# A hybrid decoder layer in float32: shared weight tiles in the branch stage, six residual buffers, and the final norm inside the expert stage

## The reference

```python
def hybrid_mixer(x, ...):
    proj = x @ w_in
    ...
    o = gated_delta_rule(q, k, v, g, beta)
    o = o * rsqrt(mean(o ** 2) + EPS) * o_norm_g * silu(z)
    branch_a = o @ w_oa
    u = glu[..., :CONF_CH] * sigmoid(glu[..., CONF_CH:])
    u = causal_depthwise_conv(u, dw_w) + dw_b
    u = silu(layer_norm(u, cln_g, cln_b))
    branch_b = u @ w_ob
    h = sigmoid(gate_a) * branch_a + sigmoid(gate_b) * branch_b
    return h @ w_o

mix = hybrid_mixer(x, ...)
x = layer_norm(ALPHA * x + mix, ln1_g, ln1_b)
ffn = routed_experts(x) + shared_expert(x)   # 64 experts, 8 for each token
x = layer_norm(ALPHA * x + ffn, ln2_g, ln2_b)
```

## Time and profile before

| | |
|---|---|
| median of 3 runs | 2569.01 us (2566.07 to 2570.61) |
| the profiled execution | 2566.55 us |
| its span, first to last instruction | 2565.0 us |
| mean granted TensorE clock | 0.967 |
| TensorE busy | 2371.6 us, 92% |
| VectorE busy | 1752.2 us, 68% |
| ScalarE busy | 1311.6 us, 51% |
| GpSimd busy | 683.8 us, 27% |

### The profile page before, as it was taken

How to read it: one execution, slowest core, us unless ns; L and a number is a source line. 1 busy time by engine, 2 the same in 40 slices (tenths; PEclk the granted TensorE clock), 3 DMA queues, 4 the chain that set the end, 5 groups by cost and what they waited for, 6 DMA issues and landing times. The chain is left out here.

```text
span 2565.0 us, 40507 instructions
## 1 busy us (share of the span) xinstructions
PE 2371.6 (92%) x11611; PEld 1933.2 (75%) x11612; DVE 1752.2 (68%) x2295; ACT 1311.6 (51%) x1714; POOL 683.8 (27%) x674
## 2 busy tenths in 40 slices
PE   7999999999999999958999786899999998999995
PEld 6777778778877888846778574788888887888782
DVE  3436898898899766638646585577667777667645
ACT  3443654654565344334412143577677776667640
POOL 2001212112211111114002213444444443444330
PEclk9999999999999999978999898999999999999998
DMA  4335454333333453263764326799989999899935
GB/s 112 52 41 82 57 65 89 62 67 75 67 61 72 100 99 91 66 234 100 218 205 151 85 73 223 262 291 328 303 281 308 320 329 341 273 295 292 330 79 219
DMA packets 244142, 435.91 MB, mean 170 GB/s; under 512 B 25096, under 2 KB 149000, under 8 KB 244046
## 3 DMA queue, kind: packets, MB, share of 16 engines
q1 hardware_dynamic: 211198, 350.70, 47.1%
q0 software_dynamic: 32848, 83.96, 12.5%
HBM read 370.88 MB, written 97.71 MB: 183 GB/s over the span
## 5 line engine op out<-in xcount | busy, mean ns | idle before, releaser
L59 PE MATMUL dn_pj<-x_hi,dn_hi 128*128 128x512 f32 x1024 | 431.4, 421 | 1.8 <-PEq L84 1.8
L61 PE MATMUL dn_pj<-x_hi,dn_lo 128*128 128x512 f32 x1024 | 403.6, 394 | 0.0
L60 PE MATMUL dn_pj<-x_lo,dn_hi 128*128 128x512 f32 x1024 | 400.5, 391 | 0.0
L59 PE MATMUL gu_ps<-e_hi,xg_hi 128*128 (+1 forms) x752 | 311.8, 415 | 0.0
L2576 DVE TENSOR_TENSOR e_lo<-e_raw,e_hi (+1 forms) x128 | 292.3, 2285 | 22.5 <-ACT e_hi L2515 22.5
L61 PE MATMUL gu_ps<-e_hi,xg_lo 128*128 (+1 forms) x752 | 296.0, 394 | 0.0
L60 PE MATMUL gu_ps<-e_lo,xg_hi 128*128 (+1 forms) x752 | 295.0, 392 | 0.0
L2515 ACT ACTIVATE e_hi<-e_raw (+1 forms) x128 | 245.1, 1916 | 46.5 <-PEq L84 35.3
L61 PEld LDWEIGHTS dn_pj<-x_hi,dn_lo 128*128 128x128 f32 x1024 | 193.0, 188 | 44.3
L59 PEld LDWEIGHTS dn_pj<-x_hi,dn_hi 128*128 128x128 f32 x1024 | 194.2, 190 | 33.7 <-issue 2.9
L60 PEld LDWEIGHTS dn_pj<-x_lo,dn_hi 128*128 128x128 f32 x1024 | 194.5, 190 | 32.0 <-issue 1.0
(11 more groups left out here) (393 smaller groups left out, 5079.0 us busy)
## 6 DMA issues: line engine op xcount, KB each, us to landing
e_raw<-in_w_gate_e_dram SPq DMA_DIRECT2D x128, 512.0 KB, 5.5
e_raw<-in_w_up_e_dram SPq DMA_DIRECT2D x128, 512.0 KB, 8.4
e_raw<-in_w_down_e_dram SPq DMA_DIRECT2D x128, 512.0 KB, 7.8
dn_raw<-in_w_in_dram SPq DMA_DIRECT2D x64, 512.0 KB
gate_rows<-qkv_next SPq DMA_DIRECT2D x16, 512.0 KB, 3.1
br_raw<-in_w_oa_dram SPq DMA_DIRECT2D x16, 512.0 KB
br_gate<-gate_rows SPq DMA_DIRECT2D x32, 256.0 KB, 4.5
br_raw<-in_w_ob_dram SPq DMA_DIRECT2D x16, 512.0 KB
```

The lines of the kernel that those rows point to most:

```text
L59: nc.tensor.matmul(out, w_hi, x_hi, start=first, stop=False)
L60: nc.tensor.matmul(out, w_hi, x_lo, start=False, stop=False)
L61: return nc.tensor.matmul(out, w_lo, x_hi, start=False, stop=last)
```

## The change

Five edits.

1. The last store of o in the delta stage is issued by SyncE, ahead of the last gate store, and SyncE waits for it to land (`o_last`). GpSimd no longer issues it or waits for it.
2. The branch stage takes w_oa for both halves first: tiles 0 to 15 are column n // 2 of half n % 2, so a weight tile serves two products in turn; then w_ob for half 0 (16 to 23) and half 1 (24 to 31), loaded for each half as before. 24 weight tiles are loaded and split instead of 32. Both halves of o are loaded and split at the start (the second into the space of the squares), u's loads come behind. The statistics' matmuls move: the means behind tiles 4 and 11, the variances behind 9 and 17 (`MEAN`, `VAR`). `br_gated_a` holds all 1024 tokens, and h is made in it and stored from it.
3. In the shared stage there are six buffers for x instead of two: four more lie in the space of the gate and up tiles' split parts. SyncE loads blocks 0 to 5 ahead; loads 6 and 7 wait for the stores of blocks 0 and 1.
4. In the expert stage the two scatters ahead of the loop go. GpSimd raises the semaphores that they raised, and two more credit writes (0.5 KB) stand in for their landing.
5. The final norm is no stage any more: its loads, sums and norm stand at the end of the experts' streams, in the space of the weights' split parts. The parameters are loaded when the last weights have been split; y's loads wait for GpSimd's word that all scatters have landed (`all_in`). There are three accumulators instead of four. `end_stage` follows at the program's end.

The diff, cut to its core:

```diff
+                sp.wait_ge(o_fin, 1 + NG * NPAIR)
+                sp.dma_start(self.o_d[(NG - 1) * GH * P:, (NPAIR - 1) * 2 * P:].rearrange("(h p) t -> p h t", p=P),
+                             ob[:].rearrange("p (h t) -> p h t", h=GH)).then_inc(o_last, 16)
                 gate_store(4 * NPAIR - 1)
+                sp.wait_ge(o_last, 16)
...
-                    if p == NPAIR - 1 and not more:
-                        o_store(g, p)
...
-                pool.wait_ge(o_stored, 16 + NG * NPAIR * 16)
+                pool.wait_ge(o_stored, NG * NPAIR * 16)
...
-            oh, uc, sq = self.o_in, self.uc, self.cln_sq
+            uc, sq = self.uc, self.cln_sq
+            oh = [self.o_in, sq]
...
-            ha = sb(ctx, "br_gated_a", [P, KT, HALF])
-            ht = [sb(ctx, f"br_h{b}", [P, HALF]) for b in range(2)]
-            rstd = [sb(ctx, f"cln_rstd{t}", [P, HALF]) for t in range(2)]
+            ha = sb(ctx, "br_gated_a", [P, KT, S])
+            rstd = [sb(ctx, "cln_rstd", [P, HALF])] * 2
...
+            A_TILES = 2 * KT
...
-                return n // (2 * KT), n // KT % 2, n % KT
...
+                if n < A_TILES:
+                    return n % 2, 0, n // 2
+                return (n - A_TILES) // KT, 1, n % KT
+
+            def weight_of(n):
+
+                return n // 2 if n < A_TILES else n - KT
+
+            def last_use(w):
+
+                return 2 * w + 1 if w < KT else w + KT
+
+            def next_weight(n):
+
+                if n < A_TILES and n % 2 == 0 or weight_of(n) + 2 >= 3 * KT:
+                    return None
+                return weight_of(n) + 2
+
+            def weight_col(w):
+
+                return (0, w) if w < KT else (1, w % KT)
+
...
+            MEAN, VAR = (4, 11), (9, 17)
+            WO, H_TILES = 2 * KT + 5, 3 * KT + 4
...
+                    if n >= NGB + A_TILES:
+                        sp.wait_ge(h_ready, n - NGB - A_TILES + 1)
+                    elif n >= NGB:
                         sp.wait_ge(ps_read, n - NGB + 1)
...
+                    sp.dma_start(self.h_d[c * P:(c + 1) * P, hs[t]], ha[:, c, hs[t]]).then_inc(h_stored[c % 2], 16)
...
-                for t in range(2):
-                    sp.dma_start(uc[:, :, hs[t]], self.uc_d[:, hs[t]].rearrange("(k p) t -> p k t", p=P)
-                                 ).then_inc(uc_in[t], 16)
+                for i in range(2):
+                    o_part(1, i)
                 gate(0)
                 gate(1)
                 for n in range(TILES):
+                    if next_weight(n) is not None:
+                        tile(next_weight(n))
                     if n + 2 < TILES:
-                        tile(n + 2)
                         gate(n + 2)
-                    if n == 3:
-                        for i in range(2):
-                            o_part(1, i)
+                    if n < 2:
+                        u_part(n)
...
+                        last = split3(nc, ps[n % 4][:], r["hi"][w % 2][:, k, :], r["lo"][w % 2][:, k, :],
+                                      src_hi[t][:, k, :], src_lo[t][:, k, :], k == 0, k == KT - 1)
                     last.then_inc(mm_done, 1)
-                    if n == 1:
-                        mean(0)
-                    elif n == VAR:
-                        var(0)
-                    elif n == VAR + 2:
-                        mean(1)
-                    elif n == KT + VAR + 1:
-                        var(1)
+                    if n in MEAN:
+                        mean(MEAN.index(n))
+                    elif n in VAR:
+                        var(VAR.index(n))
...
+                    elif n == A_TILES - 2:
+                        u_split(0, every)
...
+            spare = [nc.alloc_sbuf_tensor_at(f"sh_x{j}", [P, D], F32, offset=split_space + j * D * 4) for j in range(4)]
+            yt = [fl(x[:]) for x in wsr] + [x[:] for x in spare]
+            NY = len(yt)
...
+                def x_load(i):
+                    sp.dma_start(yt[i % NY], self.x1_d[i * P:(i + 1) * P, :]).then_inc(y_in[i % NY], 16)
+
+                for i in range(2):
+                    sp.wait_ge(w_lo, i + 3)
+                    x_load(i)
+                sp.wait_ge(mm_s, 4)
+                for e in range(2):
+                    for i in (2 * e + 2, 2 * e + 3):
+                        x_load(i)
+                    for j in range(2):
+                        if e:
+                            sp.wait_ge(self.e_in[j], 32)
+                        for n, w in enumerate((a["w_gate_e"], a["w_up_e"])):
+                            sp.dma_start(self.raw[j][:, e, n, :].rearrange("p (k f) -> p k f", k=4),
+                                         w[0, e].rearrange("(p k) f -> p k f", k=KT)[:, 4 * j:4 * j + 4, :]
+                                         ).then_inc(self.e_in[j], 16)
+                for k in range(NT):
+                    sp.wait_ge(y_add, k + 1)
+                    sp.dma_start(self.y_d[k * P:(k + 1) * P, :], yt[k % NY]).then_inc(y_out, 16)
+                    if k + NY < NT:
+                        sp.wait_ge(y_out, 16 * (k + 1))
+                        x_load(k + NY)
...
+            y = [nc.alloc_sbuf_tensor_at(f"y2_{i}", [P, D], F32, offset=w_space + i * D * 4)[:] for i in range(NT)]
+            yo = [nc.alloc_sbuf_tensor_at(f"y2_odd{i}", [P, D], F32, offset=w_space + (NT + i) * D * 4)[:]
+                  for i in range(NT)]
+            g_b, b_b = (raw[0][:, 0, n, :] for n in range(2))
+            ps = [gu[:].rearrange("p s a b -> p s (a b)"), xt[:].rearrange("p b k t -> p b (k t)"), yp[:]]
+            SUMS = len(ps)
...
+                sp.wait_ge(lo_s, E * GU)
+                sp.dma_start(g_b, a["ln2_g"][0, :].partition_broadcast(P)).then_inc(par_in, 16)
+                sp.dma_start(b_b, a["ln2_b"][0, :].partition_broadcast(P)).then_inc(par_in, 16)
+                sp.wait_ge(all_in, 1)
+                for i in range(NT):
+                    rows = slice(i * P, (i + 1) * P)
+                    sp.dma_start(y[i], self.y_d[rows, :]).then_inc(y_in[i], 16)
+                    sp.dma_start(yo[i], self.y_odd_d[rows, :]).then_inc(odd_in[i], 16)
+                for i in range(NT):
+                    sp.wait_ge(fin, i + 1)
+                    sp.dma_start(a["out"][0, i * P:(i + 1) * P, :], y[i]).then_inc(out, 16)
+                sp.wait_ge(out, NT * 16)
...
-                for n in range(2):
-                    scatter_rows(n, 0, n)
-                    scatter(n, 0, n)
+                pool.sem_inc(y_free, 2)
+                pool.sem_inc(idx_t, 2)
+                for s in range(2):
+                    pool.wait_ge(scat[s], 16)
+                    alone(pool, self.passed)
+                    pool.dma_start(self.credit_d[2 + s], self.ong[:]).then_inc(scat[s], 16)
...
+                pool.sem_inc(all_in, 1)
...
-        k.final_norm()
```

More of the change, by code:

```diff
@@ L1296, in branches @@
             st_v = [ctx.enter_context(nc.psum_tensor(f"cln_var{t}", [P, HALF], F32)) for t in range(2)]
-            o_in = [self.sems(ctx, f"o_in_sem{i}") for i in range(2)]
+            o_in = [self.sems(ctx, f"o_in_sem{i}") for i in range(4)]
             uc_in = [self.sems(ctx, f"uc_in{t}") for t in range(2)]
@@ L1343, in _, with tile @@
             def _(sp):
-                def tile(n):
-                    t, br, c = tile_at(n)
-                    if n >= 2:
-                        sp.wait_ge(r["w_ready"], n - 1)
-                    w = (a["w_oa"], a["w_ob"])[br][0, :, bass.ds(c * P, P)].rearrange("(k p) n -> p k n", p=P)
-                    sp.dma_start(r["raw"][n % 2][:], w).then_inc(r["loaded"][n % 2], 16)
+                def tile(w):
+                    br, c = weight_col(w)
+                    if w >= 2:
+                        sp.wait_ge(r["w_ready"], w - 1)
+                    src = (a["w_oa"], a["w_ob"])[br][0, :, bass.ds(c * P, P)].rearrange("(k p) n -> p k n", p=P)
+                    sp.dma_start(r["raw"][w % 2][:], src).then_inc(r["loaded"][w % 2], 16)
                 def gate(n):
                     t, br, c = tile_at(n)
-                    if n >= NGB:
+                    if n >= NGB + A_TILES:
+                        sp.wait_ge(h_ready, n - NGB - A_TILES + 1)
+                    elif n >= NGB:
                         sp.wait_ge(ps_read, n - NGB + 1)
@@ L1423, in _ @@
                     t, br, c = tile_at(n)
[L1424 removed]
+                    w = weight_of(n)
+                    pe.wait_ge(r["w_ready"], w + 1)
                     if n >= 4:
@@ L1472, in squares @@
                             act.wait_ge(var_done, 1)
+                        else:
+                            act.wait_ge(o_lo, 2 * KT)
                         A(sq[:, k, :], uc[:, k, hs[t]], ACT.Square).then_inc(sqd, 1)
@@ L1917, in shared_and_route @@
             w_in = [self.sems(ctx, f"sh_in{j}") for j in range(2)]
-            y_in = [self.sems(ctx, f"shx_in{j}") for j in range(2)]
+            y_in = [self.sems(ctx, f"shx_in{j}") for j in range(6)]
```

(24 more changed lines are left out.)

196 lines of the change are left out of this document (53 added, 143 removed).

## The result

The changed kernel takes 2537.95 us (median of four runs, 2534.98 to 2541.36) against 2569.81 for the kernel before. The ratio is 0.9879, with a 95% interval of 0.9861 to 0.9897. So it is 31.9 us faster, where 50 had been forecast, and it lies above the upper end of the range, 2535. Its profiled execution took 2541.36 us, the slowest of the four; its span is 2539.8.

A forecast was written before the change was run, and what follows sets the result against it. Each stage has its own limit; the change targets five places where TensorE stands still. Gains 3.8 + 21.5 + 8.0 + 11.5 + 5.2 = 50.0 off 2566.55 give 2516.55, plus 2.46 to the median: 2519.0; own range 2510 to 2526, with rivals 2509 to 2535.

The forecast's parts named there:

- A: End of the delta stage: SyncE's last store of o lets GpSimd's DRAIN run beside the last work; gain 3.8 us.
- C: End of the shared stage: with six buffers the residual sums follow TensorE; gain 8.0 us.
- E: Program's end: final norm's loads no longer wait for GpSimd's DRAIN and a barrier; gain 5.2 us.
- B: Branch stage: shared w_oa tiles and covered statistics sums remove TensorE's waits; gain 21.5 us, bounds 16 to 25.5.
- the floor: Branch stage: start, 32 undisturbed tiles, statistics passes and slow start; last product 193.3 us after the stage's first load.
- the late weights and h's tail: Branch stage: second-half weight tiles due every 5.6 us, allowed 0.7 us; stores and loads sharing SyncE's queue, 1.0.
- L: Branch stage: time from a weight load's issue to its landing, taken as 3.8 us.
- the ring that I priced for SyncE's queue: Branch stage, second half: weight loads behind h's stores; tile takes (4.4 + L)/2, decisive from L = 6.8; 2572 us, chance 0.02.
- GpSimd's sums: Branch stage: second variance's sums slow VectorE's low parts of u; 2.6 us put on the path.
- the rival that needed all 10.35 us: Branch stage: each sum holds VectorE up for its whole length; gain only 12, time 2528.5 us, chance 0.14.
- D: Head of the expert stage: small credit writes replace scatters, so the third block's rows come earlier; gain 11.5 us, range 5 to 13.
- that rival: Expert stage's head: credits landing after 9.2 us or more leave no gain or a loss; 2530.5 to 2533 us, chance 0.18.

The follow-up runs named there:

- experiment 3: The changed kernel, but GpSimd instead of SyncE issues the four loads of w_o, each once the part before is split: 2530.89 us (0.9854).
- experiment 5: The changed kernel, but the two small credit writes are issued in the middle of the shared stage: 2528.95 us (0.9845).
- experiment 6: The changed kernel, but with the two empty scatters ahead of the expert loop again and no late credits: 2541.24 us (0.9895).
- experiment 2: The changed kernel, but SyncE issues each store of h two tiles later: 2521.58 us (0.9808); in a second run one tile later: 2519.00 us (0.9803).

## Why the prediction was wrong

**The bound, A, C and E held.** TensorE was where the time could be won, at five places, and three of the five terms came within half a us: 3.8 against 4.2, 8.0 against 8.3, 5.2 against 5.3.

**B: the floor was right, two of the late things were wrong.** 193.3 was worked out, and 193.6 was reached once the queue was cut. The step that failed is that of the late weights and h's tail, put at 0.7 and 1.0. They cost 16 us, 14.3 more than allowed, where the last product came 16.3 late; of the rest, 2.3 is the late start. Two errors made this. First, I took L = 3.8 from one load in the middle of the stage and carried it to a place where a megabyte of w_o goes out ahead of it. In the changed kernel the weights behind the last three quarters of w_o were cast 8.2 to 8.9 us after their issue, and in experiment 3 such weights landed after 6.6 to 6.9; my own threshold was 6.8. Second, the ring that I priced for SyncE's queue had the load, the split and the gating in it, but not w_o: its landing (6.95) and split (1.92 and 2.29). The change moved w_o's four parts from tiles 18 to 24, of which the first three came while w_oa ran and no h was stored, to tiles 21 to 27, right among the stores of h. The order of the instructions showed this before any run. So the mechanism that I gave 2 in 100, for a loss of 53, came at a third of that size.

**B, GpSimd's sums: less than allowed.** VectorE's low parts of u beside the sums:

```profile
1202.19 4.62 POOL L1349 TENSOR_TENSOR cln_part<-cln_sq 128x2048 f32<-128x2048 f32 x1 [16.91 <-ACT cln_sq L1496]
1206.89 4.45 POOL L1349 TENSOR_TENSOR cln_part<-cln_part 128x1024 f32<-128x1024 f32 x2
...
1205.19 7.92 DVE L1583 TENSOR_TENSOR br_src_lo<-uc,br_src_hi 128x512 fp32r<-128x512 f32 x5
1212.43 2.49 DVE L1583 TENSOR_TENSOR br_src_lo<-uc,br_src_hi 128x512 fp32r<-128x512 f32 x4
```

Five of these took 7.92 us where four took 2.49 once the sums were over: 4.8 us lost, while the two engines' work overlapped for 6.2 (1205.19 to 1211.34). So VectorE lost most of the overlap: each of its three instructions that began beside a sum ended 0.5 to 0.6 us after that sum, about the length of one alone. The Trainium skill's page "SBUF — State Buffer" (section "SBUF: two separate sides") says that the loser fully blocks, and this agrees. It cost TensorE 0.65 in a wait, and the tile with that wait took 6.96 us in all instead of 5.6, since VectorE came to it when a third of the sums had passed. I had 2.6 for it; the rival that needed all 10.35 us did not happen.

**D: the wrong row was nearest.** The step that failed is "the nearest in place is the store; I take up to 6". The store is 512 KB issued by SyncE, the credit 0.5 KB issued by GpSimd; I had the same kind of write in the earlier trace rows with 9.2 at the least, and set it aside because of the place. In the changed kernel the two landed 9.5 to 10.0 after their issue, and in every run the writes of this name took 7.8 us or more. The place did not decide: issued in the shared stage, 44 us before the expert stage began (experiment 5), they took 8.4. Whether it is the issuer or the form of the write that makes these 8 to 10 us, no run separates. The rest of the term was right: from experiment 6 (scatters back) to experiment 5 (credits early) it is 2541.24 − 2528.95 = 12.3, where I had 11.5. My reasons for that rival were right; its chance of 0.18 was too low.

**The sum.** Of 18.9 us between forecast and median, experiment 2 gives back 16.4 and experiment 5 gives 9.0. Both together lie 5.5 below the forecast, which is about the 4 us that I had allowed in B beside the floor, and noise. Two slips in the working change nothing here: 3.7 + 2 − 3 is 2.7 and not 2.6, and the best ends as stated add up to 56.4, not 56.9, which moves the lower end of the range only.

## What to carry to other kernels

When a change moves loads in a queue that is worked off in order, list what stands in that queue at the new place, and follow each wait ahead of them round to the engine that ends it; a ring of small waits can cost most of what the change was to bring. Take the landing time of a transfer from a row with the same issuer and kind and with the same company, not from the quietest row. And cut such a ring at the queue itself: one place of distance between a store and the loads behind it gave 19 us, while easing the consumers gave nothing.

## What had not been expected of the hardware

A write of 0.5 KB that GpSimd issues took 7.8 to 14.7 us to land in the traces read here; SyncE's store of 512 KB at the shared stage's end was seen to land after 2.6. GpSimd's DRAIN at the end of a block took 3.41 us although its own transfers had been waited for just before, and 4.96 at the end of the experts. ScalarE's DRAIN at the delta stage's end took 4.09. What a DRAIN waits for the traces don't tell, but where its engine is the last one it is on the path. And the expert stage with its norm varied by 7 us (968.7 to 976.1) between the profiled executions of six programs that are alike there. TensorE's waits for `hid_lo`, the longest in that loop, differ by 2.5 us only (11.7 to 14.2), so the larger part of it has no explanation here, and a few us in this stage's length prove nothing by themselves.
